# Per-token rstd of the second norm picked from the spread row on VectorE, and a new order of the work around it

## The reference

```python
def rmsnorm(x, g):
    y = x * rsqrt(mean(x * x, axis=-1, keepdims=True) + EPS)
    return y * g

h = x + hgrn2_mixer(rmsnorm(x, ln_g[0]), ...)        # layer 0
u = rmsnorm(h, ln_g[1])                               # the norm in question
for g, (window, dilation) in enumerate(((128, 1), (512, 4), (2048, 16))):
    q, k, v = (u @ w_in[:, 3*g*W + i*W : 3*g*W + (i+1)*W] for i in range(3))   # W = 2048, 16 heads of 128
    ...                                               # banded attention per group
h = h + (merged * silu(u @ w_gate)) @ w_out
out = rmsnorm(h, final_g)
```

## Time and profile before

| | |
|---|---|
| median of three runs | 1660.09 us (1658.81 to 1661.02) |
| the profiled execution | 1658.73 us |
| its span, first to last instruction | 1656.9 us |
| mean granted TensorE clock | 0.996 |
| stretch of the change (first k = 6 matmul of group 0 due, to the eleventh of group 1) | 546.1 to 564.9 us |

### The profile page before, as it was taken

The page is one execution under the profiler, slowest core; times in us unless marked ns, Lnnn a source line. Parts: engine busy times, 40 slices in busy tenths (PEclk is TensorE's granted clock), DMA queues, the critical chain, the costliest instruction groups (busy, mean ns, idle before and its releaser), DMA issues.

```text
span 1656.9 us, 22106 instructions
## 1 busy us (share of the span) xinstructions
PE 1632.1 (99%) x8251; PEld 1391.6 (84%) x8251; DVE 809.9 (49%) x1410; ACT 645.8 (39%) x1098; POOL 20.8 (1%) x40
## 2 busy tenths in 40 slices
PE   7999999999999999999999999999999999999997
PEld 5888888888887798888898888899888889888886
DVE  6674675575577534444323444433344432444445
ACT  4553453453454433333332343332333332243333
POOL 0000000000000000000000000000000000000000
PEclk9999999999999999999999999999999999999999
DMA  6523223223321333333333334323323332433311
GB/s 212 168 77 102 76 76 91 86 76 89 87 79 52 92 100 96 84 83 63 98 102 90 96 83 96 71 78 114 92 60 92 96 70 89 116 95 85 81 52 64
DMA packets 247998, 149.47 MB, mean 90 GB/s; under 512 B 47040, under 2 KB 227648, under 8 KB 247920
## 3 DMA queue, kind: packets, MB, share of 16 engines
q1 hardware_dynamic: 203328, 139.69, 30.5%
q0 software_dynamic: 2608, 8.39, 1.5%
q10 hardware_dynamic: 41984, 0.27, 1.3%
HBM read 146.02 MB, written 6.50 MB: 92 GB/s over the span
## 4 chain that ended last, share of the span: by engine, by line
PE 95%; DVE 2%; ACT 1%; issue 0%; DMA 0%; SPq 0%; DVEq 0%; ACTq 0%
PE proj L440 81%; PE inner L731 3%; PE inner L440 2%; PE inner L699 2%; PE inner L719 2%; PE inner L687 1%; PE inner L601 1%; PE inner L624 1%; PE inner L627 1%; PE inner L613 1%; PE inner L606 0%; DMA v<-x 0%; DVE v L1521 0%; DVE rows L1127 0%; DVE hT L1287 0%
## 5 line engine op out<-in xcount | busy, mean ns | idle before, releaser
L1087 DVE TENSOR_TENSOR w_lo<-raw,w_hi 128x1024 fp32r<-128x1024 f32 x252 | 307.9, 1223 | 463.7 <-ACT w_hi L780 462.6
L440 PE MATMUL proj<-u_hi,w_hi 128*128 128x512 f32 x1280 | 509.3, 398 | 0.0
L440 PE MATMUL proj<-u_hi,w_lo 128*128 128x512 f32 x1280 | 499.8, 390 | 0.0
L440 PE MATMUL proj<-u_lo,w_hi 128*128 128x512 f32 x1280 | 498.5, 389 | 0.0
L780 ACT ACTIVATE w_hi<-raw 128x1024 fp32r<-128x1024 f32 x252 | 265.0, 1053 | 125.2 <-PE proj L440 117.0
L440 PEld LDWEIGHTS proj<-u_hi,w_lo 128*128 128x128 f32 x1280 | 240.2, 188 | 52.1
L440 PEld LDWEIGHTS proj<-u_lo,w_hi 128*128 128x128 f32 x1280 | 240.7, 188 | 48.2
L440 PEld LDWEIGHTS proj<-u_hi,w_hi 128*128 128x128 f32 x1280 | 240.5, 188 | 47.5 <-issue 0.2
L440 PE MATMUL proj<-w_hi,u_hi 128*128 128x512 f32 x440 | 177.5, 403 | 5.8 <-DVE u_lo L1107 3.0
L440 PE MATMUL proj<-w_lo,u_hi 128*128 128x512 f32 x440 | 174.7, 397 | 0.0
L440 PE MATMUL proj<-w_hi,u_lo 128*128 128x512 f32 x440 | 174.6, 397 | 0.0
(11 more groups left out here) (172 smaller groups left out, 1498.8 us busy)
## 6 DMA issues: line engine op xcount, KB each, us to landing
raw<-at_w_in SPq DMA_DIRECT2D x160, 512.0 KB, 4.1
raw<-hg_w_in SPq DMA_DIRECT2D x64, 512.0 KB, 4.2
raw<-hg_w_out SPq DMA_DIRECT2D x16, 512.0 KB, 3.5
raw<-at_w_out SPq DMA_DIRECT2D x16, 512.0 KB, 4.6
v<-x SPq DMA_DIRECT2D x4, 512.0 KB, 6.4
bias_tiles<-ext_rows POOLq DMA_DIRECT2D x1, 2048.0 KB, 11.8
bias_tiles<-ext_rows POOLq DMA_DIRECT2D x2, 1024.0 KB, 17.6
bias_n<-bias_tiles POOLq DMA_DIRECT2D x16, 128.0 KB, 4.3
```

Source lines behind the costliest of these rows:

```text
L440: ins = nc.tensor.matmul(bank[:, :], stationary(a), moving(b), start=(first and n == 0), stop=(last and n == 2))
L1087: nc.vector.tensor_tensor(w["lo"][:, slot, :], raw[:, slot, :], w["hi"][:, slot, :].bitcast(F32), ALU.subtract).then_inc(w_ready, 1)
```

## The change

- PE: `token_sum` and its semaphore are gone. `feature_sum` keeps its place before k = 7 and waits for the last addition of squares instead of for ACT. The first step of group 1 into each rotating bank leaves out of its wait the counts that the copies of group 0 give; the first step into inner[4] waits until ACT's Ln has read p_ss.
- ACT: the Ln and Exp for the columns are gone. The rounds of tiles 4, 5, 6 stand ahead of the Ln and Exp for the row, the round of tile 7 behind it. The four copies of group 0 stand behind the first and the second pair of u_high, two each, and wait for the columns from DVE.
- DVE: w_lo of tiles 4, 5, 6, then a wait for the row of rstd, two multiplies of the row by the identity (in natural order, and reading the row with a step of four), each 128 x 512, two sums over 128 columns each into the columns of rstd, then w_lo of tile 7 and the norm. y_f and eg hold the products in between; they are free at that time.

```diff
 # value_step (PE)
                 if k == 0 and layer is AT and value_bank(layer, None, e) is proj[bank]:
-                    pe.wait_ge(bank_free[bank], before)
+                    in_inner = sum(layer.event(None, i)[1] == bank for i in range(ST))
+                    pe.wait_ge(bank_free[bank], before - in_inner)
+                elif k == 0 and layer is AT and group:
+                    pe.wait_ge(rstd_step, 1)
...
-            def token_sum():
-                pe.wait_ge(sq_added, KT - 1)
-                for i in range(2 * ST):
-                    tokens = slice(i * P, (i + 1) * P) if i < ST else slice(i - ST, S, RES)
-                    ins = nc.tensor.matmul(p_ss[:, i:i + 1], sq_sum[:, tokens], ones[:, 0:1], start=True, stop=True)
-                ins.then_inc(token_sums, 1)
-
             def feature_sum():
-                pe.wait_ge(rcol_step, 1)
+                pe.wait_ge(sq_added, KT - 1)
                 nc.tensor.matmul(p_ss[:, :], ones[:, :], sq_sum[:, :], start=True, stop=True).then_inc(feature_sums, 1)
...
             for k in range(KT):
-                if k == KT - 2:
-                    token_sum()
                 if k == KT - 1:
                     feature_sum()
...
 # ACT
+            def raw_value_events():
+                for i in range(ST):
+                    if i == ST - 1:
+                        for s in range(ST):
+                            copy_values(AT, None, 1, ST + s)
+                    u_high(1, 2 * i)
+                    u_high(1, 2 * i + 1)
+                    split_hi(AT, None, 4 + i, False)
+                    if i == 0:
+                        act.wait_ge(rcol_ready, 1)
+                    if i < 2:
+                        copy_values(AT, None, 0, 2 * i)
+                        copy_values(AT, None, 0, 2 * i + 1)
...
-            act.wait_ge(token_sums, 1)
-            nc.scalar.activation(cols[:, 0:2 * ST], p_ss[:, 0:2 * ST], ACT.Ln, scale=1.0 / D, bias=eps[:, :])\
-                .then_inc(rcol_step, 1)
-            act.wait_ge(rcol_step, 1)
-            nc.scalar.activation(cols[:, 8:8 + 2 * ST], cols[:, 0:2 * ST], ACT.Exp, scale=-0.5).then_inc(rcol_ready, 1)
+            for n in range(3):
+                split_hi(AT, None, n, False)
             act.wait_ge(feature_sums, 1)
             nc.scalar.activation(rstd[:, :], p_ss[:, :], ACT.Ln, scale=1.0 / D, bias=eps[:, :]).then_inc(rstd_step, 1)
             act.wait_ge(rstd_step, 1)
             nc.scalar.activation(rstd[:, :], rstd[:, :], ACT.Exp, scale=-0.5).then_inc(rstd_ready, 1)
-            act.wait_ge(rcol_ready, 1)
-            first_value_events(AT, 0)
-            first_value_events(AT, 1)
+            split_hi(AT, None, 3, False)
+            raw_value_events()
             value_events(AT, None, 2, 0)
...
 # DVE
-            for n in range(4):
+            for n in range(3):
                 split_lo(AT, None, n, False)
+            dve.wait_ge(rstd_ready, 2)
+            picked = (y_f, eg)
+            for i, row in enumerate((rstd[:, :].rearrange("p (t n) -> p t n", t=ST),
+                                     rstd[:, :].rearrange("p (n r) -> p r n", r=RES))):
+                nc.vector.tensor_tensor(picked[i][:, :].rearrange("p (t n) -> p t n", t=ST), row,
+                                        ident[:, :].unsqueeze(1).broadcast_to([P, ST, P]), ALU.mult).then_inc(rcol_step, 1)
+            for i in range(2):
+                dve.wait_ge(rcol_step, i + 1)
+                ins = nc.vector.tensor_reduce(cols[:, 8 + ST * i:8 + ST * (i + 1)],
+                                              picked[i][:, :].rearrange("p (t n) -> p t n", t=ST), AX.X, ALU.add)
+            ins.then_inc(rcol_ready, 1)
+            split_lo(AT, None, 3, False)
             norm(1)
```

More of the change, by code:

```diff
@@ L241, in program @@
         raw_hi_ready, raw_ready = sems("raw_hi_ready raw_ready")
-        sq_ready, sq_added, token_sums, feature_sums = sems("sq_ready sq_added token_sums feature_sums")
+        sq_ready, sq_added, feature_sums = sems("sq_ready sq_added feature_sums")
         rcol_step, rcol_ready, rstd_step = sems("rcol_step rcol_ready rstd_step")
@@ L499, in value_step, with feature_sum @@
                     ins.then_inc(value_tile_done, 1)
-            def token_sum():
+            def feature_sum():
                 pe.wait_ge(sq_added, KT - 1)
-                for i in range(2 * ST):
-                    tokens = slice(i * P, (i + 1) * P) if i < ST else slice(i - ST, S, RES)
-                    ins = nc.tensor.matmul(p_ss[:, i:i + 1], sq_sum[:, tokens], ones[:, 0:1], start=True, stop=True)
-                ins.then_inc(token_sums, 1)
-            def feature_sum():
-                pe.wait_ge(rcol_step, 1)
                 nc.tensor.matmul(p_ss[:, :], ones[:, :], sq_sum[:, :], start=True, stop=True).then_inc(feature_sums, 1)
@@ L833, in _, with first_value_events @@
             nc.scalar.activation(param[:, 0:3 * H], param[:, 0:3 * H], ACT.Exp).then_inc(lb_exp, 1)
-            def first_value_events(layer, group):
+            def first_value_events(layer):
                 for i in range(3):
[L837 to L840, removed]
+                    split_hi(layer, None, i, False)
                 for s in range(ST):
[L842 to L846, removed]
+                    copy_values(layer, None, 0, s)
+                split_hi(layer, None, 3, False)
+            def raw_value_events():
[11 more added lines that the diff above has]
+                        copy_values(AT, None, 0, 2 * i + 1)
             def value_events(layer, q, group, first):
@@ L859, in _ @@
             nc.scalar.activation(ones_r[:, :], ones[:, :], ACT.Copy).then_inc(ones_r_ready, 1)
-            first_value_events(HG, 0)
+            first_value_events(HG)
             def kT_copy(g):
```

## The result

The changed kernel takes 1649.34 us, median of four executions (1647.56 to 1650.58), against 1660.01 us of the kernel before over four (1658.81 to 1661.02): ratio 0.9938, 95% interval 0.9926 to 0.9949. That is faster by 0.6%, and the interval lies clear of the 0.2% under which nothing can be told. Predicted were 1650.0 us, range 1647.0 to 1654.0. The profiled execution took 1648.23 us (span 1646.4, clock 0.997).

The account below looks back on a forecast made before the run. TensorE, busy 99% of the span, was taken to bound the kernel. Savings of 5.84 + 4.25 = 10.09 us, the rest 0, gave 1648.6 us for the profiled execution and 1650.0 us on the median, range 1647.0 to 1654.0.

Parts of the forecast that it names:

- Part 1: PE before and in k=6: wait 1.36, one-column products 2.77 and lower clock 1.71 us go, 5.84 us saved.
- rival B: Gaps go but PE's clock still falls once, perhaps from narrow or fp32 work: costs 1.3 to 1.7 us, 1651.5 us; chance 6%.
- Part 2: PE before group 1: earlier rounds and relaxed bank wait remove the 2.95 us gap and 1.30 us of low clock, 4.25 us.
- clock term: Group 1's first ten matmuls take 2.35 instead of 3.65 us with no gap before them: 1.30 us saved.
- Part 3: Two multiplies and two sums on DVE for the rstd columns, 2.7 us in all, stay hidden from PE: 0 us.
- The second pick: DVE's multiply by the identity reading rstd with a 16-byte step: sized like the contiguous one, 0.68 us.
- The margin: Time to spare before ACT's u_hi would wait for DVE's first normed row: 2.5 us.
- the 8 us before PE sees a delay: The picks on DVE can be about 8 us late before PE's group 2 sees it.
- Part 4: ACT's four copies of group 0 moved behind the first two pairs of u_hi: cost 0 us.
- A: Second gap stays because something other than the copy holds group 1: only 5.84 us won, 1654.3 us; chance 4%.
- D: PE stands before k=6 or k=7 for another input, so little is won: about 1657 us; chance 3%.
- C: Picks or DVE's order hold the norm, PE stands before group 2: 1663 us if picks are 21 us late; chance 2%.

Follow-up runs that it names:

- e1: Changed kernel with the eight one-column products and their wait for the last addition back before k=6, results unread: 1654.57 us, ratio 0.9971.
- e2: Changed kernel with only the wait for the last addition of squares back before k=6, no products: 1650.89 us, ratio 0.9949.
- e3: Changed kernel with eight one-column products of the block of ones before k=6, no wait, results unread: 1651.13 us, ratio 0.9946.
- e9: Changed kernel with 24 one-column products of the block of ones before k=6, no wait, results unread: 1657.07 us, ratio 0.9989.
- e4: Kernel before with only the rounds of tiles 4 to 6 moved ahead of Ln and Exp and group 1's bank wait relaxed: 1655.87 us, ratio 0.9975.
- e6: Changed kernel with all four rounds behind Ln and Exp, bank wait still relaxed: 1649.88 us, ratio 0.9945.
- e5: Changed kernel with group 0's four copies back ahead of tile 7's round and group 1 waiting for its bank's whole count: 1654.07 us, ratio 0.9968.
- e10: Same kernel as e5, another execution for its trace: 1653.31 us.
- e12: Kernel before, no edit, one more execution for its trace: 1658.50 us.
- e11: Changed kernel with six more DVE multiplies behind the picks (contiguous, stepped read, stepped write, twice over): 1646.57 us, one execution.
- e7: Changed kernel with ten more 128x512 multiplies on DVE behind the picks, delaying the norm: 1649.50 us, ratio 0.9938.
- e8: Changed kernel with thirty more 128x512 multiplies on DVE behind the picks, delaying the norm: 1664.47 us, ratio 1.0032.

## Why the prediction was right

- **Part 1, 5.84 us.** Right in every term: e1 puts them back at 1.35, 2.77 and 4.43 us. What it left open, which of the two lowers the clock (rival B), e2, e3 and e9 answer in part: the gap of 1.35 us alone does not (e2), 1.81 us of products alone do not (e3), and a longer run of narrow products does (e9). The old 2.77 us of products without the gap stay untested.
- **Part 2, 4.25 us.** The gap of 2.95 us went, by e4 without part 1 too. In the kernel before, the copies ended last, as said, but ACT had the rounds ahead of them, and by the estimate at e4 moving the rounds alone would nearly have closed this gap. The reading of the earlier trace rows, two releasers for one stand, was worth the care: with the bank wait relaxed and the rounds in their old place, 0.9 us of stand are left (e6), and with the rounds ahead but the bank wait whole, the copies hold PE for 3.0 us (e5). These 3.0 us are new ones, since there the copies wait for the picks. The prediction did not say that the relaxed wait pays for the picks rather than for the old gap.
- **Its clock term, 1.30 us**, was taken as fixed. The prediction had "no window here falls without a gap just before it" and made the converse of it silently: that this gap costs clock in every execution. e5 and e10 show a gap of 2.98 us at 1.00. Both traces of before (the second is e12) have the loss, so the sum against the profiled execution holds (10.07 us measured in the stretch, 10.09 predicted). Whether other executions of before escape the loss is not shown.
- **Part 3, 0 us.** Right in effect. The second pick was mis-sized, 1.07 instead of 0.68 us, because the nearest row was an ACT copy from PSUM, where the step costs nothing. The trace after shows 1.07 us, e11 1.08 us. The rule of the Trainium skill, "SBUF — State Buffer", section "Door 1: The DMA port swizzle", pointed the right way: a penalty for each access to a new 16-byte line, though here of 1.56 times and not the 4 that I made of it as an estimate. The margin was read right: 2.3 us were left of the 2.5. So were the 8 us before PE sees a delay: e7 is 7.3 us late and costs nothing, and in e8, 21.8 us late, group 2 begins 14.1 us later, so 7.7 us are covered.
- **Part 4, 0 us.** ACT's copies cost nothing: ACT waits for PE ahead of the first three pairs of u_hi and of the copies of group 1 (572.62), and PE never stands.
- **Rivals.** A did not come (no stand at 551.98). B did not: clock 1.00. But its suspicion of narrow work was right, and the ground against it, that a stretch without a gap stays at 1.00, does not hold in general: e9 has no gap and falls to 0.52. D did not: k=6 went at once. C is real as a mechanism: e8 is slower than before, 15.5 us above the change, where the prediction had 13 us for picks 21 us late. Its price lacked the lower clock behind the stands, and its first place was wrong: w_lo of tile 7 is missed before the norm is.

## What to carry to other kernels

Where one engine is busy 99% of the span, look for the few microseconds in which it does nothing or narrow work, and price them in full: wait, work, and the slower matmuls behind. If a stand has two releasers in the waits, ask of each why it is late: one may only stand behind the other in a queue. Then ask again with the new work in place, which can make the other one late for a new reason (e5). Work moved to an engine with idle time is free as long as what is queued behind it has a margin, and the margin is to be worked out for each instruction behind it, the nearest first.

## What the runs showed of the hardware

- One-column products keep TensorE "busy" in the profile and can still cost it its clock: 6.2 us of them without a gap were followed by matmuls at 0.43 us instead of 0.23 (e9); 1.8 us of them (e3) and a gap of 1.35 us (e2) were not; the two in sequence, 4.1 us, were in all four traces that had them (before, e12, e1, e4).
- A gap of about 3 us (2.8 to 3.0 us idle) cost clock in two traces of one kernel (before, e12: 0.56 and 0.55 behind it) and not in two of another (e5, e10: 1.00). A single profile of such a gap does not say what it costs elsewhere.
- A VectorE multiply of 128x512 fp32 takes 0.69 us contiguous and 1.08 us when either its read or its write in SBUF has a step of 16 bytes (e11; the pick with the stepped read took 1.07 us in the change).
- The weight loads of the one-column fp32 products began 0.11 us apart from contiguous tokens and 0.24 us apart from tokens with a step of four (before, line 506).
